# Position biases moved to SP, DVE and two rounds of flips, start-up loads reordered, two operand turns moved to a scan step's start, and a store by tile

## What is computed

```python
def first_block(x, ln_attn_g, w_in, qk_norm_g, diff_lambda, diff_subln_g, w_out,
              ln_ffn_g, w_up, conv_w, conv_b, w_down, rel_bias):
    for i in range(DEPTH):
        h = rms_norm(x, ln_attn_g[i])
        dq, dk, dv, mq, mk, mv = jnp.split(h @ w_in[i], cuts, axis=-1)   # 1024 x 3072
    ...
        x = x + jnp.concatenate([y_diff, y_moba], axis=-1) @ w_out[i]
        x = x + conv_ffn(rms_norm(x, ln_ffn_g[i]), w_up[i], conv_w[i], conv_b[i], w_down[i])
    return x
...
    def step(state, inp):                  # rwkv7_scan, over the tokens in either direction
        r_t, w_t, k_t, v_t, kk_t, a_t = inp
        sa = jnp.einsum('bhvk,bhk->bhv', state, -kk_t)
        state = (state * w_t[:, :, None, :] + sa[..., None] * (kk_t * a_t)[:, :, None, :]
                 + v_t[..., None] * k_t[:, :, None, :])
        return state, jnp.einsum('bhvk,bhk->bhv', state, r_t)
...
    bias = rpb[:, dr[:, None, None, :, None], dc[None, :, :, None, :]]   # neighbourhood_attention
    s_lat = s_lat + bias.transpose(1, 2, 0, 3, 4, 5).astype(jnp.float32)
    s_lat = jnp.where(col_ok[:, None, :, None, :], s_lat, NEG_INF)
...
def sqrelu_mlp(u, w1, w2):
    return jnp.square(jax.nn.relu(u @ w1)) @ w2
```

## Time and profile before

| | |
|---|---|
| time, median of 3 runs | 2091.5 us (2087.97 to 2093.78) |
| the profiled execution | 2088.72 us |
| its span, first to last instruction | 2086.9 us |
| busy: PE, DVE, ACT, POOL | 1930.2, 1132.6, 868.3, 223.4 us |
| mean granted TensorE clock | 0.963 of full speed |

### The profile page before, as it was taken

How to read it: one execution, slowest core, us unless ns; L and a number is a source line. 1 busy time by engine, 2 the same in 40 slices (tenths; PEclk the granted TensorE clock), 3 DMA queues, 4 the chain that set the end, 5 groups by cost and what they waited for, 6 DMA issues and landing times. The chain is left out here.

```text
span 2086.9 us, 36823 instructions
## 1 busy us (share of the span) xinstructions
PE 1930.2 (92%) x15696; PEld 1612.7 (77%) x15696; DVE 1132.6 (54%) x1790; ACT 868.3 (42%) x1539; POOL 223.4 (11%) x257
## 2 busy tenths in 40 slices
PE   5997999899899999989999998899999979888998
PEld 4746998685699878856888887688888668577986
DVE  4565675465567655456556565444344445436643
ACT  4344564345456543445322234322232243545532
POOL 1100122020012200101212211200000011000000
PEclk9998999999899999999999998999999999998999
DMA  7574565468456542235000031523233214014653
GB/s 251 176 274 139 162 184 181 141 199 304 141 151 189 176 153 90 91 127 162 24 4 3 4 124 59 137 86 98 84 101 96 67 61 131 31 41 129 192 185 121
DMA packets 231610, 264.54 MB, mean 127 GB/s; under 512 B 14182, under 2 KB 153750, under 8 KB 231063
## 3 DMA queue, kind: packets, MB, share of 16 engines
q1 hardware_dynamic: 222023, 259.23, 39.0%
q10 hardware_dynamic: 9424, 2.95, 0.8%
HBM read 261.07 MB, written 1.09 MB: 126 GB/s over the span
## 5 line engine op out<-in xcount | busy, mean ns | idle before, releaser
L401 PE MATMUL acc<-rounded,rounded 128*128 128x512 f32 (+1 forms) x2552 | 880.9, 345 | 33.2 <-DVE rounded L653 11.0
L402 PE MATMUL acc<-rounded,rounded 128*128 128x512 f32 (+1 forms) x2552 | 874.8, 343 | 0.0
L403 PE MATMUL acc<-rounded,rounded 128*128 128x512 f32 (+1 forms) x2552 | 874.0, 342 | 0.0
L385 DVE TENSOR_TENSOR rounded<-arena,rounded 128x2048 fp32r<-128x2048 f32 (+1 forms) x194 | 435.0, 2246 | 298.6 <-ACT rounded L374 298.5
L401 PEld LDWEIGHTS acc<-rounded,rounded 128*128 128x128 f32 x2552 | 488.0, 191 | 102.4 <-issue 28.8
L403 PEld LDWEIGHTS acc<-rounded,rounded 128*128 128x128 f32 x2552 | 487.3, 191 | 60.7
L402 PEld LDWEIGHTS acc<-rounded,rounded 128*128 128x128 f32 x2552 | 488.1, 191 | 59.3 <-issue 0.2
L374 ACT ACTIVATE rounded<-arena 128x2048 fp32r<-128x2048 f32 (+1 forms) x194 | 362.8, 1872 | 357.8 <-PE acc L403 321.0
L1982 PE MATMUL sc<-arena 64*64 64x64 f32 x2560 | 98.9, 225 | 14.3 <-DVE arena L2128 12.7
L1982 PEld LDWEIGHTS sc<-arena 64*64 64x64 f32 x2560 | 87.1, 138 | 24.1 <-DVE arena L2128 15.8
L1399 DVE SCALAR_TENSOR_TENSOR arena<-acc,pcol,arena 128x254 f32<-128x254 f32 (+1 forms) x176 | 76.8, 478 | 51.2 <-ACT arena L1380 49.7
(11 more groups left out here) (244 smaller groups left out, 1709.3 us busy)
## 6 DMA issues: line engine op xcount, KB each, us to landing
arena<-in_w_ff SPq DMA_DIRECT2D x64, 1024.0 KB, 5.4
arena<-in_w_ada SPq DMA_DIRECT2D x48, 1024.0 KB, 5.2
arena<-in_w_up SPq DMA_DIRECT2D x88, 512.0 KB, 5.1
arena<-in_w_in SPq DMA_DIRECT2D x24, 1024.0 KB, 5.2
arena<-in_w_down SPq DMA_DIRECT2D x20, 1024.0 KB, 5.1
arena<-in_w_out SPq DMA_DIRECT2D x16, 1024.0 KB, 5.2
arena<-in_w_in_even SPq DMA_DIRECT2D x9, 1024.0 KB, 5.4
arena<-in_w_in_odd SPq DMA_DIRECT2D x8, 1024.0 KB, 5.2
```

The source lines that it names most:

```text
L385: dve.tensor_tensor(r32(w), w, r32(high_slot(c)[:, 0:size(c)]), ALU.subtract).then_inc(split_made, 1)
L401: pe.matmul(ps, ah, bh, start=first, stop=False)
L402: pe.matmul(ps, ah, bl, start=False, stop=False)
L403: return pe.matmul(ps, al, bh, start=False, stop=last)
```

## The change

Five edits.

- **Start.** x comes in two DMAs with a semaphore each. Chunk 0 stands ahead of the parameters. Six of the twelve parameter rows are issued by ACT, six by SP behind chunk 0; the lambda rows and constants stand behind chunk 3. ACT and DVE do all of the first norm and split chunks 0 to 2 before lambda, exponential and SiLU. The two bias products stand behind QKV's first column block, on `sc` banks. That block goes by chunk first, then by token tile. The table for the first attention's bias (`t5_sync_dma`) goes through memory ahead of chunk 8 and not of chunk 4.
- **Scan.** The turns of direction 0 stand ahead of level 1 and those of direction 1 in levels 2 and 3, on PE and on ACT.
- **Position biases.** SP issues the 32 loads, eight each ahead of the first chunk of `ff2(1)` to `ff2(4)`. PE mirrors four banks in each of the rounds `ff2(5)` and `ff2(7)`, one ahead of each token tile of the first block. DVE adds the mask on the way out of PSUM; POOL and ACT have no part.
- **Last round.** ACT's copies and PE's eight products in a row are gone from the second block.
- **Store.** Each token tile of the output is stored by a DMA of its own.

```diff
             if l == 0:
-                stage("bcast", acc=1)
-                stage("t5", acc=1)
+                stage("bcast", sc=1)
+                stage("t5", sc=1)
             stage(("qkv", l), acc=12, tr=8)
...
-            sp.dma_start(h_lat[:, :, :], I["x"][0].rearrange("(t p) d -> p t d", p=P)).then_inc(x_landed, 16)
+            for tt in range(TT):
+                sp.dma_start(h_lat[:, tt, :], I["x"][0, tt * P:(tt + 1) * P, :]).then_inc(x_landed[tt], 16)
             sp.dma_start(keep[:, 0:P], consts[0][:, 0:P]).then_inc(ident_landed, 16)
-            param_dmas(sp, [0], params_landed)
+
+        def setup_sync_dma(sp):
             sp.dma_start(lrow[0:1, 0:2 * 4 * HD], I["diff_lambda"].rearrange("(o l) a b -> o (l a b)", o=1)).then_inc(rows_landed, 16)
...
-                if cb == 0:
+                if cb == 0 and l:
                     order = [(k0, tt) for tt in range(TT) for k0 in (0, 4)]
...
+                if l == 0 and cb == 0:
+                    setup_bias_pe(pe)
...
+            for d, i in TURNS[:2]:
+                turn(d, i)
             for lev in range(1, LEVELS):
                 for d, q in enumerate(scans):
...
-                if lev <= len(TURNS):
-                    turn(*TURNS[lev - 1])
+                if lev in (2, 3):
+                    turn(*TURNS[lev])
...
+            for d, i in TURNS[:2]:
+                keep_turned(d, i)
...
-                if lev <= len(TURNS):
-                    keep_turned(*TURNS[lev - 1])
+                if lev in (2, 3):
+                    keep_turned(*TURNS[lev])
...
+                        if not hf and key in NEAR_ROUNDS:
+                            near_dve(dve, NEAR_ROUNDS.index(key), t)
...
-                        if hf and t == 2:
-                            near_act(act, range(0, 1))
                         if hf and t >= 2:
                             norm_square(act, following, t - 2)
-                        if hf and t == 2:
-                            near_act(act, range(1, 8))
...
-            def last_round(block, k0, n):
-                if block == 1 and n == 2:
-                    near_pe(pe)
-                if block == 1 and n == 3:
-                    norm_turn(pe, ("mix", 1, 1), 0)
+            def among(key):
+                def place(block, k0, n):
+                    if block == 0 and key in NEAR_ROUNDS:
+                        near_pe(pe, NEAR_ROUNDS.index(key), n)
+                    if block == 1 and n == 3 and key == ("ff2", EIGHTHS - 1):
+                        norm_turn(pe, ("mix", 1, 1), 0)
+                return place
...
-                if e == 0:
-                    near_dma(act)
-                elif e < EIGHTHS:
+                if 0 < e < EIGHTHS:
                     tok_walk(act, ahead_act, ("ff2", e - 1), ET, 2)
...
+        def near_dma(sp, qt, i):
+
+            if qt == 1 and i == 0:
+                sp.wait_ge(tr_full, tr_at[("norm", ("ff", 0, 0))] + 4)
...
+            r = 2 * qt + i
+            for h in range(8):
+                src = bass.AP(tensor=rpb.tensor, offset=(h * nd + NA_KH - 1 - r) * nc_ + NA_KW - 1 - (GRID_W - 1),
+                              ap=[[1, GRID_W], [nc_, 4], [1, GRID_W]])
+                sp.dma_start(hankels[qt][i * GRID_W:(i + 1) * GRID_W, h, :].rearrange("p (t k) -> p t k", t=4), src)\
+                  .then_inc(near_landed[qt], 16)
...
-        def near_pool(pool):
-            pool.wait_ge(near_landed, 16 * 32)
-            for i in range(8):
-                rows = hankels[i // 4][:, 2 * (i % 4):2 * (i % 4) + 2, :]
-                win = const("near")[:, (i // 4) * SEQ:(i // 4 + 1) * SEQ].unsqueeze(1).broadcast_to([P, 2, SEQ])
-                pool.tensor_tensor(rows, rows, win, ALU.add).then_inc(near_windowed, 1)
-
-        def near_pe(pe):
-            pe.wait_ge(near_windowed, 8)
-            for i in range(8):
-                ps = claim(pe, "sc", sc_at["near"] + i)
-                pe.matmul(ps[:, :], flip64, near_rows(hankels, i), start=True, stop=True).then_inc(sc_full, 1)
+        def near_pe(pe, again, n):
+
+            qt = 1 - again
+            if n == 0:
+                pe.wait_ge(near_landed[qt], 16 * 16)
+            ps = claim(pe, "sc", sc_at["near"] + 4 * again + n)
+            pe.matmul(ps[:, :], flip64, near_rows(hankels, 4 * qt + n), start=True, stop=True).then_inc(sc_full, 1)
 
...
+        def near_dve(dve, again, n):
+
+            qt, f = 1 - again, sc_at["near"] + 4 * again + n
+            win = const("near")[:, qt * SEQ:(qt + 1) * SEQ].unsqueeze(1).broadcast_to([P, 2, SEQ])
+            pair = lambda v: v.rearrange("p (a b) -> p a b", a=2)
+            dve.tensor_tensor(pair(near_rows(near, 4 * qt + n)), pair(filled(dve, "sc", f)[:, :]), win, ALU.add).then_inc(drain("sc", f), 1)
...
             first_sync_dma(sp)
             for g in range(len(chunks)):
                 if g == 1:
+                    param_dmas(sp, [0], params_landed, slice(6, None))
+                if g == RAW:
                     setup_sync_dma(sp)
-                if g == RAW:
                     later_sync_dma(sp)
+                if g == 2 * RAW:
                     t5_sync_dma(sp)
...
+                for n, e in enumerate(range(1, 5)):
+                    if g == chunk_at[("ff2", e)]:
+                        near_dma(sp, 1 - n // 2, n % 2)
...
-            ff1.updated(sp)
-            sp.dma_start(out.rearrange("(t p) d -> p t d", p=P), h_lat[:, :, :]).then_inc(out_stored, 16)
-            sp.wait_ge(out_stored, 16)
+            for tt in range(TT):
+                ff1.updated(sp, 0, tt)
+                sp.dma_start(out[tt * P:(tt + 1) * P, :], h_lat[:, tt, :]).then_inc(out_stored, 16)
+            sp.wait_ge(out_stored, 16 * TT)
...
+            param_dmas(act, [0], params_landed, slice(0, 6))
             norm_squares(act, first_norm(0, "attn"))
             ahead_act(act, 0)
-            setup_bias_act(act)
+            wait_drained(act, "tr", tr_at["params"])
             norm_highs(act, first_norm(0, "attn"))
             ahead_act(act, HIGH - 1)
+            setup_bias_act(act)
...
-            lambda_dve(dve)
-            setup_dve(dve)
             for l in range(DEPTH):
-                norm_dve(dve, first_norm(l, "attn"))
                 if l == 0:
+                    for tt in range(TT):
+                        norm_scale(dve, first_norm(l, "attn"), tt)
+                    setup_dve(dve)
                     ahead_dve(dve, 0)
+                    wait_drained(dve, "tr", tr_at["params"])
+                norm_dve(dve, first_norm(l, "attn"), scaled=1 - l)
+                ahead_dve(dve, chunk_at[("qkv", l)] + HIGH - 1)
+                if l == 0:
+                    lambda_dve(dve)
                     setup_bias_dve(dve)
-                ahead_dve(dve, chunk_at[("qkv", l)] + HIGH - 1)
                 qkv_dve(dve, l)
```

More of the change, by code:

```diff
@@ L92, in constants @@
     in_window = np.where((kc >= start) & (kc < start + NA_KW), 0, NEG).astype(f)
-    keep["near"] = tile(in_window.reshape(SEQ // GRID_W, GRID_W, SEQ)[:, ::-1].reshape(SEQ, SEQ))
+    keep["near"] = tile(in_window)
     first["flip"] = eye[::-1]
@@ L955, in first_and_second_block, with param_dmas @@
         sub_gain = stats(DEPTH)
-        def param_dmas(eng, groups, landed):
+        def param_dmas(eng, groups, landed, part=slice(None)):
             eng.wait_ge(params_cleared, 2 if groups[-1] else 1)
             for g in groups:
-                r = 0
-                for name, n in PARAM_GROUPS[g]:
+                for i, (name, n) in list(enumerate(PARAM_GROUPS[g]))[part]:
+                    r = sum(rows for _, rows in PARAM_GROUPS[g][:i])
                     src = I[name]
```

57 lines of the change are left out of this document (22 added, 35 removed).

## The result

The changed kernel takes 2056.7 us (median of 4 runs, 2055.5 to 2060.8) against 2091.3 before (2088.0 to 2093.8): a ratio of 0.983, 95% interval 0.981 to 0.986. Over all runs of this study it is 2059.6 (16 runs) against 2090.8 (32 runs), 31 us less; one further execution of the kernel before, of 4743 us, is left out. The profiled execution took 2060.8 (span 2058.9), the slowest of its four; the spans of the others are 2053.7 to 2055.0.

What follows compares the result with a forecast made beforehand. PE was taken as the bound, with gains only where it idles or has a slow clock. 12.0 + 10.6 + 0 + 7.8 + 1.3 = 31.7 took 2088.7 to 2057.0, or 2059.8 as median; forecast 2058, range 2050 to 2068.

Steps and rivals of the forecast that it cites:

- Start, -12.0: Kernel start: QKV begins at 16.3 us and its second block at 30.2 instead of 42.2; bounds -13.3 and -9.7.
- Bias loads, -10.6: Position-bias loads: PE wins waits of 5.51 and 3.05 us and 2.0 us of slow clock; bounds 8.6 to 11.
- Flips and the last round, 0: FFN rounds: eight flips cost 7 us in earlier rounds and leave the last; net 0, ends -4 and +3.
- Scan, -7.8: Scan: reordered turns fill PE's wait, 6.0 us over eight steps, plus 1.8 us of slow clock; 4 to 9.3.
- 0.75 a step, 6.0 for eight: Scan: each of eight steps wins 0.75 us by moved turns; bounds 0.5 and 0.98 a step.
- I expect that gone: 1.8: Scan: the slow clock that followed the step-start stall in two steps disappears, winning 1.8 us.
- Store, -1.3: Output store: only half of it remains behind the last update, winning 1.3 us; bounds 0 to 2.0.
- SP becomes the bound: Bias loads, rival: eight small loads ahead of a weight load hold SP beyond its slack; 2095 and more, chance 0.02.
- constants bind the start: Start, rival: `keep` lands at 34 us, PE idles 5 us and gets a slow clock; 2065, chance 0.08.
- The scan gives nothing: Scan, rival: `x_set` comes late by the moved turns, or levels 1 and 4 wait in full; 2066, chance 0.1.
- More than forecast: Last round and start, rival: the round keeps its clock and the landing is early; 2051, chance 0.06.
- It does not reach the end: Whole kernel, rival: some later wait has a fixed time, so gains are lost; 2088, chance 0.02.

Runs made afterwards that it cites:

- products_first: Changed kernel with the two bias products back ahead of QKV in PE's queue, chunk 0 still early: 2073.0 us.
- chunk0_late: Changed kernel with chunk 0 issued behind eight more small loads on SP, the bias products still behind QKV's first block: 2060.1 us.
- loads_on_act: Changed kernel with the small position-bias loads issued by ACT again, masks still on DVE: 2069.2 us (2063.3 to 2075.7).
- all_flips_idle: Changed kernel with all eight flips moved into PE's idle times and the scan's step 0 turns behind its levels as before: 2047.0 us.
- scan_back: Changed kernel with the four turns of each scan step back behind levels 1 to 4, on PE and ACT: 2063.4 us.
- split_late: Changed kernel with the last round's flips in PE's idle time and one weight chunk's split behind DVE's chain: 2055.6 us without the profiled run's disturbance.

## Why the prediction was right

It said 2058 (2050 to 2068); the median is 2056.7. Point by point:

- **Start, -12.0:** measured -11.7. QKV at 16.44 where 16.3 was said, the second block at 30.68 where 30.2 was. Chunk 0 was used at 9.32, not 8.8; the two bias products took 1.05 us (29.63 to 30.68), not 0.9. The constants did not bind. What the sum did not say is the share of each edit: the products' place is worth 10.1 of it (products_first); chunk 0's place is worth 1.7 at QKV's start for the 3.75 us that were tried (chunk0_late), and the rest of its way was not.
- **Bias loads, -10.6:** measured -11.3, inside 8.6 to 11 but for 0.3. The second wait's cause was given as DVE running late beside POOL's additions; loads_on_act shows that it was those additions, 3.2 us, while ACT's lateness is the other 8.1. The small loads on SP cost the rounds nothing: 286.8 with them on SP and in loads_on_act without them, and 280.0 in all_flips_idle, with them and without the flips. Whether a small load ahead of a weight load on one queue delays its landing, as the prediction allows for, is not put to the test: they were issued over 4 us ahead of it.
- **Flips and the last round, 0:** measured -0.6 (+6.8 and -7.4; 0.85 us a flip). The idle of 8 us and the clock of 0.78 behind it came as said. "7 us in the earlier rounds" was right, and the experiments show that it need not have been paid.
- **Scan, -7.8:** measured -5.6; this term was mis-sized, within its bounds of 4 to 9.3. The wait per step fell as said (1.50 to 0.84, and a step takes 25.7 us instead of 26.5), and steps 1 to 7 won 8.0 us (188.1 to 180.1, slow steps included). The step that failed is "0.75 a step, 6.0 for eight": step 0 is no such step. There the turns came to stand ahead of a drain of `yTB`, with a wait of 1.84 us in this profile and 2.80 in the two others, and step 0 lost 2.4 us (58.1 to 60.5) instead of winning 0.75. "I expect that gone: 1.8" came true: before has two slow stretches in steps 1 to 7, no profile with the new order has one, and scan_back, with the old order, has one again. The upper bound was added up wrong: eight times 0.98 and 1.8 make 9.6, not 9.3.
- **Store, -1.3:** measured -1.4, and +1.4 with one DMA again.
- **The sum:** 31.7 was said; the changed places give 30.6 in the first profile, and 31 between the medians over all runs. That the first four runs' median came within 1.3 us of the forecast is closer than either can be trusted, and in part luck: the changed kernel's runs go from 2055.5 to 2065.3 with the clock, and the scan's miss of 2.2 us is offset in part by the 0.7 and 0.6 that the bias loads and the last round gave more than said. Over all 16 runs the median is 2059.6, close to the 2059.8 that the sum gives and that was put at 2058.

Of the rivals, "SP becomes the bound" and "constants bind the start" are shown false by the windows and the timeline. "The scan gives nothing" is false, though its worry about things queued ahead was near what step 0 did, on PE instead of ACT. "More than forecast" did not come: the last round lost its clock (0.77 from load 242 to 243). "It does not reach the end" is false.

Still open: a kernel with the flips in the idle time, the split behind DVE's chain, and ACT's squares ahead of its copies. The 3.70 us wait would be gone there and DVE's chain would start 2.5 us earlier (3.0 instead of 5.5 us behind load 242, as in split_late); whether the projection behind it then waits for the split was not tried.

## What to carry to other kernels

Work that PE can do at any time belongs where PE waits, not between products where it is the bound: eight small products cost 6.8 us in one place and next to nothing in another; but look at what is queued on the engine that empties the banks. When a step of a loop is reordered, look at its first pass by itself: its neighbours are others. And an instruction with two SBUF inputs on DVE must be priced by what POOL does at that time.

## What the runs showed of the hardware

POOL's additions make each DVE operation of two SBUF inputs 0.9 us longer, whatever its size (1.57 instead of 0.68 us, 3.18 instead of 2.29), and leave its copies out of PSUM alone (2.47 and 2.48 for four). A group's mean hides it: for 128x512 it is 1283 and 1355 ns, because operations with and without POOL beside them are mixed in it.

PE's granted clock differs between executions of one kernel over the same code (0.69 and 0.80 in the same window), and the time of the kernel before goes with it, over 18 us.

There is a slowdown that the granted clock does not show. In two profiles, of split_late and of the changed kernel's third, the second layer's up projection was some 14 us longer. (The profile of split_late has some 10 us more behind load 250, in a stretch of 27 us at a granted clock of 0.50.) Windows of the second and the third profile of the changed kernel:

```profile
600.00:700.00 100.00, 100.00 (x803) 97.89 (x803) 69.06 (x86) 61.79 (x90) 30.91 (x42) 1.00 0.64 189
```

```profile
600.00:700.00 100.00, 100.00 (x753) 100.00 (x752) 62.87 (x78) 53.17 (x80) 21.98 (x31) 1.00 0.57 161
```

PE is busy throughout and its clock is given as full, but weight loads there come 6.40 us instead of 5.68 (in_w_up, two issues each), and the queues move 161 GB/s instead of 189. These two executions took 2073.5 and 2076.5 us. What causes it stays open.
